# Two edits to a decoder-layer kernel: who copies and who scales in the dilated attention, and in which order the experts stand

## The reference

```python
def moe(h, w_router, b_router, w_up, b_up, w_down, b_down):
    ...
    logits = (hf @ w_router + b_router).astype(jnp.float32)
    top_val, top_idx = lax.top_k(logits, TOP_K)
    gate = jax.nn.softmax(top_val, axis=-1)
    ...
    group_sizes = jnp.zeros((N_EXPERTS,), jnp.int32).at[flat_e].add(1)
    up = lax.ragged_dot(xs, w_up, group_sizes) + b_up[e_sorted]
    down = lax.ragged_dot(clamped_swiglu(up), w_down, group_sizes) + b_down[e_sorted]
    out = jnp.zeros_like(hf).at[tok].add(down * g_sorted[:, None].astype(down.dtype))

def dilated_attention(q, k, v):
    ...
    for window, dil in DIL_CONFIGS:         # ((128, 1), (512, 4), (2048, 16))
        ...
        o, lse = band_attention(split(q)[:, :, None], split(k), split(v), window // dil)
    w = jax.nn.softmax(jnp.stack(lses, axis=0), axis=0)
    return jnp.einsum("cbsh,cbshd->bshd", w.astype(q.dtype), jnp.stack(outs, axis=0))
```

## Time and profile before

| | |
|---|---|
| three runs | 1482.35, 1484.19, 1487.72 us |
| the profiled execution | 1487.72 us, of which its span 1485.9 |
| busy share of the span | PE 90%, DVE 43%, ACT 21%, POOL 13% |
| PE's granted clock over the span | 0.968 |
| moved by DMA | 506.02 MB, mean 341 GB/s |
| expert matmuls L1871 and L1891 | 584.9 and 308.4 us |

### The profile page before, as it was taken

One profiled execution on the slowest core, in us unless ns is written; L12 is line 12 of the kernel. 1 busy time (PEld: TensorE's weight loads), 2 busy tenths in 40 slices (PEclk: granted clock), 3 DMA queues, 4 the chain that ended last, 5 costly groups with the idle time before them and its releaser, 6 DMA issues.

```text
span 1485.9 us, 44835 instructions
## 1 busy us (share of the span) xinstructions
PE 1335.0 (90%) x18595; PEld 776.0 (52%) x18602; DVE 645.0 (43%) x1704; ACT 315.4 (21%) x840; POOL 188.5 (13%) x265
## 2 busy tenths in 40 slices
PE   5999999999978999988989978899999999989973
PEld 2464555655545555554555544455555555545531
DVE  2558446785562433333333323243344334333344
ACT  2120014664320121111212111112111211111211
POOL 0300003443000010000101000001000100010131
PEclk9999999999988999999999989999999999999996
DMA  9758308302469999999999999999899899999995
GB/s 354 269 204 290 123 0 331 151 1 113 185 257 422 407 402 423 424 425 426 426 425 407 409 426 427 424 426 405 352 427 426 331 400 426 425 425 425 424 384 192
DMA packets 77344, 506.02 MB, mean 341 GB/s; under 512 B 9596, under 2 KB 16228, under 8 KB 52728
## 3 DMA queue, kind: packets, MB, share of 16 engines
q1 hardware_dynamic: 66624, 474.96, 77.9%
q0 software_dynamic: 6560, 20.00, 3.6%
q10 hardware_dynamic: 4120, 10.51, 1.8%
HBM read 473.90 MB, written 31.53 MB: 340 GB/s over the span
## 4 chain that ended last, share of the span: by engine, by line
PE 63%; DMA 28%; DVE 4%; issue 2%; another core or an unknown queue 1%; SPq 1%; ACT 1%; POOL 0%; ACTq 0%; DVEq 0%; POOLq 0%
PE ps L1871 25%; DMA arena<-in_w_down 24%; PE ps L1891 14%; PE ps L1528 7%; PE ps L1784 4%; DMA arena<-in_w_in 2%; PE ps L1636 2%; PE ps L1675 2%; PE ps L1715 1%; PE ps L1495 1%; PE ps L1879 1%; DVE arena L910 1%; DMA arena<-in_w_ada 1%; PE ps L1643 1%
## 5 line engine op out<-in xcount | busy, mean ns | idle before, releaser
L1871 PE MATMUL ps<-arena 128*32 128x256 f32 x10240 | 584.9, 382 | 39.6 <-issue 28.5
L1871 PEld LDWEIGHTS ps<-arena 128*32 128x32 f32 x10240 | 342.0, 111 | 259.6 <-issue 53.6
L1891 PE MATMUL ps<-arena 128*32 128x256 f32 x5120 | 308.4, 392 | 42.4 <-DMA arena<-in_w_down 42.4
L1350 DVE TENSOR_SCALAR arena<-ps 128x128 f32<-128x128 f32 x160 | 46.8, 292 | 578.3 <-PE ps L1879 573.3
L1891 PEld LDWEIGHTS ps<-arena 128*32 128x32 f32 x5120 | 157.9, 112 | 169.0 <-issue 53.6
L825 ACT ACTIVATE arena<-ps 32x256 f32<-32x256 f32 x320 | 120.1, 375 | 330.0 <-PE ps L1891 309.4
L819 ACT ACTIVATE arena<-arena 128x128 f32<-128x128 f32 x160 | 49.7, 311 | 519.2 <-DVE arena L1350 519.2
L603 POOL DMA_INDIRECT arena<-xn_rows,arena x81 | 78.9, 974 | 482.3 <-DVE arena L1320 396.3
L1528 PE MATMUL ps<-arena 128*128 128x512 f32 (+1 forms) x320 | 129.7, 561 | 3.1 <-DMA arena<-in_w_in 3.1
L1528 PEld LDWEIGHTS ps<-arena 128*128 128x128 f32 x320 | 60.3, 192 | 64.0 <-issue 56.1
L589 POOL TENSOR_SCALAR arena<-arena 128x128 f32<-128x128 f32 (+3 forms) x48 | 51.7, 1082 | 223.3 <-DVE arena L1122 201.6
(11 more groups left out here) (328 smaller groups left out, 977.8 us busy)
## 6 DMA issues: line engine op xcount, KB each, us to landing
arena<-in_w_up SPq DMA_DIRECT2D x128, 2048.0 KB, 16.9
arena<-in_w_down SPq DMA_DIRECT2D x64, 2048.0 KB, 29.2
arena<-in_w_ada SPq DMA_DIRECT2D x12, 2048.0 KB, 11.5
slot_rows<-arena SPq DMA_DIRECT2D x4, 3328.0 KB, 25.6
arena<-in_w_in SPq DMA_DIRECT2D x5, 2048.0 KB, 10.8
slot_rows<-arena ACTq DMA_DIRECT2D x80, 128.0 KB, 6.1
arena<-in_w_o SPq DMA_DIRECT2D x2, 2048.0 KB, 11.0
arena<-in_x SPq DMA_DIRECT2D x4, 512.0 KB, 5.2
```

Source lines behind the costliest of these rows:

```text
L1871: ins = pe.matmul(out_of(y, g), xgT[:, 2 * n + k, :], tiles[par][n][:, k, at:at + 256], start=(n == 0 and k == 0), stop=False)
L1891: ins = pe.matmul(out_of(5, g), actT[:, y, k, :], tiles[par][4 + y][:, k, 256 * g:256 * (g + 1)], start=False, stop=(y == 1 and k == 3))
```

## The change

There are two edits.

The first is in the dilated units. The scaling of half h = 1 goes from POOL to DVE: in `sums(u)` it stands right behind the reciprocal and waits for that. It signals a new semaphore, `scaled_dve`. The copy of the transposes goes to ACT for both halves, in one instruction, and DVE has no copy there any more. PE's waits follow: `turn` waits for `scaled_dve`, and `copied` for `pt_act` alone. The sparse units are as they were.

The second replaces the table `rank_at`. With the token counts of the inputs both tables give 80 chunks.

```diff
--- before.py
+++ after.py
@@ -42,7 +42,7 @@
 
 def part_of_ranks():
 
-    rank_at = [27, 24, 10, 5, 30, 14, 4, 21, 16, 1, 20, 13, 8, 26, 9, 2, 23, 11, 7, 19, 17, 0, 22, 15, 6, 28, 12, 3, 29, 18, 25]
+    rank_at = [20, 29, 9, 2, 27, 15, 6, 24, 18, 1, 21, 12, 8, 23, 10, 3, 30, 11, 5, 28, 17, 0, 26, 13, 7, 25, 16, 4, 22, 14, 19]
     rank_at = [rank_at[0] + 1, 0] + [r + 1 for r in rank_at[1:]]
     start, split = np.zeros(N_EXP), np.zeros(N_EXP)
     for x, rank in enumerate(rank_at):
@@ -324,8 +324,8 @@
                              "hid_sb", "cv_ps", "cv_sb")]
         sc_ps, sc_in, sc_exp, pc_ready, pc_tr, pc_sb = [
             sem(n) for n in ("sc_ps", "sc_in", "sc_exp", "pc_ready", "pc_tr", "pc_sb")]
-        qk_done, neg_ready, exp_done, scl_ready, scaled_act, scaled_pool = [
-            sem(n) for n in ("qk_done", "neg_ready", "exp_done", "scl_ready", "scaled_act", "scaled_pool")]
+        qk_done, neg_ready, exp_done, scl_ready, scaled_act, scaled_pool, scaled_dve = [
+            sem(n) for n in ("qk_done", "neg_ready", "exp_done", "scl_ready", "scaled_act", "scaled_pool", "scaled_dve")]
         tr_done, pt_dve, pt_act, pv_done, o_ev, o_sq = [
             sem(n) for n in ("tr_done", "pt_dve", "pt_act", "pv_done", "o_ev", "o_sq")]
         sq_added, osum_ps, orstd_ready, y_nsa, y_sum, yg_ready = [
@@ -583,11 +583,12 @@
 
 
             for u, (ty, pr, rows) in enumerate(units):
-                pool.wait_ge(scl_ready, u + 1)
-                for n, (i, at) in enumerate(rows):
-                    pb = probs[:, u % 4, 1, span(i, at)]
-                    ins = pool.tensor_scalar(pb, pb, scl[:, u % 4, 2 * n + 1:2 * n + 2], None, ALU.mult)
-                ins.then_inc(scaled_pool, 1)
+                if ty != N_DIL:
+                    pool.wait_ge(scl_ready, u + 1)
+                    for n, (i, at) in enumerate(rows):
+                        pb = probs[:, u % 4, 1, span(i, at)]
+                        ins = pool.tensor_scalar(pb, pb, scl[:, u % 4, 2 * n + 1:2 * n + 2], None, ALU.mult)
+                    ins.then_inc(scaled_pool, 1)
                 if u - 4 in pair_last:
                     add_squares(pair_last[u - 4])
             add_squares(6)
@@ -775,7 +776,7 @@
                     w = width(u)
                     act_e.wait_ge(tr_done, u + 1)
                     act_e.wait_ge(pv_done, u - 1)
-                    act_e.activation(pT[:, u % 2, 0, 0:w], ps[:, 4, 0:w], ACT.Copy).then_inc(pt_act, 1)
+                    act_e.activation(pT[:, u % 2, :, 0:w], ps[:, 4:6, 0:w], ACT.Copy).then_inc(pt_act, 1)
                 if u + 3 < UNITS:
                     exps(u + 3)
                 if u + 2 < UNITS:
@@ -1109,11 +1110,19 @@
                                                          ALU.mult, ALU.add, lsum[:, n:n + 1])
                     link(ins)
                 if u >= 4:
-                    v.wait_ge(scaled_pool, u - 3)
+                    if u - 4 < DIL_U:
+                        v.wait_ge(scaled_pool, u - 3)
+                    else:
+                        v.wait_ge(scaled_dve, u - 3 - DIL_U)
                     v.wait_ge(scaled_act, u - 3)
                 dst = scl[:, u % 4, 0:width_s]
                 if ty == N_DIL:
                     v.reciprocal(dst, ls).then_inc(scl_ready, 1)
+                    v.wait_ge(scl_ready, u + 1)
+                    for n, (i, at) in enumerate(rows):
+                        pb = probs[:, u % 4, 1, span(i, at)]
+                        ins = v.tensor_scalar(pb, pb, dst[:, 2 * n + 1:2 * n + 2], None, ALU.mult)
+                    ins.then_inc(scaled_dve, 1)
                 else:
                     link(v.reciprocal(dst, ls))
                     i = rows[0][0]
@@ -1122,12 +1131,13 @@
                     v.tensor_tensor(both, both, gates, ALU.mult).then_inc(scl_ready, 1)
 
             def pt_evac(u):
+                if units[u][0] == N_DIL:
+                    return
                 w = width(u)
                 v.wait_ge(tr_done, u + 1)
                 if u >= 2:
                     v.wait_ge(pv_done, u - 1)
-                h = 1 if units[u][0] == N_DIL else 0
-                v.tensor_copy(pT[:, u % 2, h:2, 0:w], ps[:, 4 + h:6, 0:w]).then_inc(pt_dve, 1)
+                v.tensor_copy(pT[:, u % 2, :, 0:w], ps[:, 4:6, 0:w]).then_inc(pt_dve, 1)
 
             def pair_out(pr):
 
@@ -1660,12 +1670,16 @@
 
             def copied(u):
 
-                pe.wait_ge(pt_dve, u + 1)
-                if u >= DIL_U:
+                if u < DIL_U:
+                    pe.wait_ge(pt_dve, u + 1)
+                else:
                     pe.wait_ge(pt_act, u - DIL_U + 1)
 
             def turn(u):
-                pe.wait_ge(scaled_pool, u + 1)
+                if u < DIL_U:
+                    pe.wait_ge(scaled_pool, u + 1)
+                else:
+                    pe.wait_ge(scaled_dve, u - DIL_U + 1)
                 pe.wait_ge(scaled_act, u + 1)
                 if u >= 1:
                     copied(u - 1)
```

## The result

In 20 runs each, the changed kernel has a median of 1491.20 us (1485.08 to 1494.98) and the kernel before 1482.66 us (1476.18 to 1487.72). The ratio is 1.0055, 95% interval 1.0044 to 1.0067. The forecast was 1484 us: 1491.20 lies inside the range given, but the change is clear of noise and has another sign than the forecast's sum.

The account below looks back on a forecast made before the run. Loads of the expert weights were taken to set the pace; +1.5 (attention) + 10.2 (end of experts) + 0.5 (shared DMA) - 12.5 (tail) = -0.3 us, so 1484 us against a median of 1484.19; range 1475 to 1492.

Parts of the forecast that it names:

- part B: Behind the last expert: a two-chunk last part lets final fetches start earlier, so PE goes on 12.5 us sooner.
- Holes, -0.6 us: Expert weight loads: new holes of 3.6 and 2.4 us, old ones of 5.4 and 1.2 closed; last tile 0.6 us earlier.
- The second chunk, T' = T + 10.2: End of experts: a whole second chunk behind the last tile adds 10.85, less 0.6; bounds +7.5 and +12.
- T': End of the last expert matmul in the changed kernel, forecast 10.2 us later than before.
- T: End of the last expert matmul in the kernel before, 1433.97 us in its profile.
- The tail of the changed kernel: Behind the experts: release at T' + 5, first last fetch T' + 9.5, PE goes on T' + 13.7, then 25.7 us unchanged.
- the credit with the release fixed: Tail: if the last chunk's release stays 13.4 us behind its matmul, the saving is 4.4 us instead of 12.5.
- Early fetches beside the last weights, 0.5 us: End of experts: first fetches share DMA with the last weight tiles, charged 0.5 us; queue turns could add up to 3.3.
- Attention, +1.5: Dilated attention: waits for ACT's later 512-wide copy outweigh vanished POOL waits, about +1.5 us, bounds -3 and +3.
- The port pair: Dilated attention: DVE's scalings could stand still beside POOL's addition of squares, adding 3.8 us at three meetings; outside the sum.
- rival 1: Tail: last chunk's release fixed at 13.4 us behind its matmul, saving only 4.4 us; 1492 us, chance 0.24.

Follow-up runs that it names:

- e5: Kernel before with two ranks of the old table exchanged, so part 26 has one chunk instead of two and part 41 two instead of one: 1.0012.
- e12: Changed kernel run unaltered for a third trace, on the same chip as the third trace of the kernel before: 1.0052.
- e11: Kernel before run unaltered for a third trace: median 1479.49 us, ACT's copy of the last chunk 0.2 us late.
- e3: Kernel before run unaltered for a second trace: ACT's copy of the last chunk 12.1 us late, tail 51.2 us.
- e4: Changed kernel run unaltered for a second trace: 1.0039, tail 33.8 us.
- e9: Changed kernel with the ranks of places 26 and 41 exchanged back, so part 26 has two chunks and the last part one: 1.0032.
- e15: Kernel before with parts 26 and 41 exchanged, and the residual load waiting until the first of the last four fetches has landed: 1.0021.
- e1: Kernel before with the attention edit alone, old expert order kept: 1.0005.
- e13: Kernel before with half the attention edit: ACT copies both halves, scaling stays on POOL: 1481.60 us, one run.
- e16: Kernel before, one run for a trace on a further chip: ACT's copy of the last chunk 10.3 us late, tail 48.7 us.
- e18: Changed kernel with a quarter of the bytes in each early fetch, one run: copy of the chunk before the last 8.4 us late, 96 matmuls 13.1 us.
- e17: Kernel before with the 12 early fetches also waiting for PE's last expert matmul, one run: ACT's copy 0.17 us late.
- e14: Kernel before with the other attention half: DVE scales the second half and keeps its copy: 1491.99 us, one run.

## Why the prediction was wrong

**The step that failed is part B's credit of 12.5 us for the tail, which rests on its account of the last chunk's release.** It took the 13.4 us of the earlier trace rows as part of the kernel before, let them shrink to 5 in the changed kernel at no price to PE, and carried the sum over to the median of the runs. On two chips of five (e5 to e12) none of eight traces has the hold; in six of them the fetches stand beside PE's work, so that it could have shown. Like against like, the tail gives back 7.2 us, or it gives back 17.4 and PE loses 18.6:

- *Without a hold (e11 to e12).* The end of the experts is 12.6 us later behind the start, the tail 7.2 shorter (45.1 to 37.9). PE gets the last fetch's rows 19.0 us behind the end in e11 (1453.29), not 26.2, because POOL's own row of 12 fetches lets the thirteenth go only 12.3 us behind the end. With 1.56 us of attention this is 12.56 - 7.24 + 1.56 = +6.9 of the +8.4 between the spans; the other 1.5 lie ahead of the experts, where starts of one kernel differ by up to 4 us.
- *With a hold (e3 to e4).* The tail shrinks by 17.4 (51.2 to 33.8), more than forecast, but what held one signal up in the old kernel now stalls PE in its second chunk: the end is 18.6 us later, not 12. The sum is 18.6 - 17.4 + 1.6 = +2.8, and +4.9 between the spans.

The pair that I had, and then got, crosses the two: a hold before (51.9) and none after (37.8). That is why the profiled executions agree with the sum to 0.6 us while the medians don't.

The other steps, one by one:

- *Holes, -0.6 us.* (The first one's own terms, 603.1 - 599.6, give 3.5 and not 3.6.) The sum is right, -0.6 in the first pair and 0.0 in e11 to e12, though not each part: 1.1 instead of 2.4 at 635, and 2.0 at 1168 not foreseen; that the whole came out is luck in part. e9 and e5 show the two sides apart, +4.8 and -4.9.
- *The second chunk, T' = T + 10.2.* 12.0 in the first pair, at the upper bound of +12 that was given. The missing 1.8 us are the clock (granted 0.50 from 1433 to 1437): PE now waits 3.46 us for the last tile instead of 1.27, because part 37 has one chunk less, and the 32 matmuls behind that wait take 3.40 us for 1.94; the first of the next chunk take 5.70 for 5.39. I had written that PE might reach part 41 earlier and wait, and had not priced the wait; the waits of 3.08 and 2.96 us in the earlier trace rows, with 3.53 and 3.57 us of matmuls behind them, show its price.
- *The tail of the changed kernel.* Forecast T' + 39.4 (13.7 + 25.7), measured 37.8 and 37.9. The release at T' + 5 was wrong (T' + 0.2), and so were the 4.5 us from there to POOL's first last fetch (8.8, so T' + 8.9 for T' + 9.5); the two nearly cancel. The landing was right, 4.3 us for 4.2, and PE goes on at T' + 13.2 for T' + 13.7, with 24.6 us behind it for 25.7. What the 8.8 us hold is the write behind the residual load: from its issue to POOL's fetch it takes 7.0 and 6.9 us where the load goes out 1 us ahead of it (the changed kernel, e12), and 2.7 where the load went out 10.5 us ahead (e4) or goes later (e15). And the credit with the release fixed is, by the prediction's own terms (13.4 + 4.5 + 4.2 = 22.1), 4.1 us and not 4.4.
- *Early fetches beside the last weights, 0.5 us.* The first fetch was issued at 1426.15 and the last tile still came on time. By the Trainium skill's rule of turns between the two kinds of queue ("DMA: Bandwidth & Descriptors", section on SWDGE, HWDGE and iDMA) the tile would have come up to 3.3 us late. The trace doesn't decide it: 12 fetches of 0.5 MB take some 15 us at 410 GB/s, and the DMA engines are full until 1446 (0.37 from there to 1449), so by this estimate the fetches moved hardly any data before 1431, with the last tile there at 1432.7.
- *Attention, +1.5.* The number came out, +1.56, and the mechanism named is there: ACT's copy of the 512-wide unit is late for the next pair (0.82 to 0.84 us a pair; 0.7 to 0.8 forecast). But the number is luck. The terms given, three times 0.3, 0.9 for the first unit and -0.7 in the drain, add up to 1.1; the pairs cost 0.77, 0.73 and 0.71 us instead of 0.3, the first unit nothing of its own, and only the drain's -0.65 is as forecast, though PE waits there as well (1.07 us on ACT).
- *The port pair.* DVE's scalings took 0.487 and 0.420 us (0.48 and 0.42), but none of them stood beside an addition of POOL, so they say nothing of the lock. What did stand there is DVE's multiply L1109, which reads two inputs from SBUF: 1.17 us for 0.55 at 324.68, inside POOL's addition of 324.17 to 325.43, and 1.21 beside that of 345.23. By "SBUF — State Buffer" in the Trainium skill, section on the two separate sides, such an instruction and one of GpSimd that reads SBUF exclude each other for a whole instruction; the trace agrees. It cost PE nothing that shows: its waits at the three pairs' first units are 0.84, 0.82 and 0.82 us, with such an addition at the first and the third and none at the second.

Of the rivals, 1 gave the right size (1492) for a wrong reason: its release was to be as late in the changed kernel as before, and the traces have it prompt, or turned into lost time of PE. Nothing in one trace could have told me which executions have the hold. That the profiled one was the slowest of three doesn't tell it either: e1's was the quickest of its 12 runs and has the hold. But the one unexplained row was the largest credit in the sum. Priced with the hold on both sides (rival 1's -4.4) the sum was +7.8; without it on either, the credit is the 19.0 us of e11 less the forecast's 13.7, 5.3 us, and the sum +6.9.

No version was faster than the kernel before; nearest are e1 (1.0005) and e5 (1.0012), at its level. What stays open: why some chips show the hold and others not (each of the five was seen in one set only), and by what path POOL's run of fetches delays PE's signals.

## What to carry to other kernels

When a large credit in a sum rests on a wait whose releaser the profile can't name, work the sum out with the wait on both sides and on neither; a credit that exists only when one side has it belongs to the execution and not to the change. Ask for a second trace, from another chip, before such a wait is counted: here all traces of two chips lacked it, and the time of the profiled execution among its fellows told nothing. And an engine that was idle during a disturbance hides it; giving it work there, as a second chunk in the last part does, turns a late signal into lost time.

## What the runs showed of the hardware

- On three chips (e1 to e4, e13 to e15, e16 and e18), and in the first trace of before, PE's signal was 4.8 to 13.3 us late, and where PE had work its 96 matmuls took 13.0 to 15.7 us instead of 5.4 to 5.7, with gaps put down to issue (3.2 to 5.6 us in all) and a lower clock behind them, while POOL issued a row of 12 indirect transfers at 1.25 us each; in the eight traces of two other chips there was nothing of it. Moving the row behind PE's signal removed it (0.17 us, e17); a quarter of the bytes did not (e18, DMA share 0.34).
- The kernel before ran at medians of 1478.3 and 1478.9 us on the chips without it, 1484.3 and 1484.5 on two with it: 6 us. That the hold makes this difference isn't shown: its tails with the hold are 48.7 to 51.9 us against 45.1, but those of e1 and e13, with the shorter holds of 6.4 and 4.8 us, are 45.9.
- What a wait of PE costs beyond itself: behind waits of 2.96 to 3.46 us its next 32 matmuls took 3.2 to 3.6 us (and 3.40 behind 3.46 above, at a granted clock of 0.50), behind 2.39 us 1.94; it was 2.92 behind 2.78 in e16 and 3.38 behind 2.80 in e14.
- A DVE instruction with two inputs in SBUF took 1.17 and 1.21 us instead of 0.55 beside POOL's addition of 1.26 us (the changed kernel, 324.68 and 345.70).
